# A transposed block's activations and remainders in one 512-column matmul, the halves added on VectorE

## The chip, the cores and the metric

The program runs on one core of one Trainium2 chip. The metric is the device time of that core in microseconds (us): 3461.25 us as the median of 3 runs of the kernel before. Engines are named as in the profile: PE is TensorE's matmul, PEld its weight load, DVE is VectorE, ACT is ScalarE, POOL is GpSimd, SP is SyncE, which only issues DMAs here.

## What is computed

Two transformer blocks on 256 tokens of width 2048, all in fp32. Cut to the matrix products that matter here:

```python
u = rms_norm(h, g_mix_pre) @ w_in               # 2048 x 5120: q, k, v, xr, yg
rec = rglru_bidirectional(xr, conv_w, ...) * gelu(yg)
s = einsum(q * HEAD_DIM ** -0.5, k) + bias      # attention of the first block
h = h + rms_norm(concat(norm(attn), norm(rec)) @ w_out)
ff = (silu(fn @ w_ffn_gate) * (fn @ w_ffn_up)) @ w_ffn_down      # 5632 hidden
...                                             # a gated embedding, then the second block
h2 = xn @ w_in_2; x = x + mixed @ w_out_2
qry = xn @ peer_w_query                         # routing: 16 of 16384 experts, 8 heads
act = gelu(xn . expert_down[idx])               # all 16384 experts are multiplied here
out = sum(gate * act * expert_up[idx])
```

The kernel doesn't gather experts: it multiplies the tokens with all 16384 rows of expert_down, applies gelu, multiplies by a gate that is zero for an expert not chosen, and multiplies with all of expert_up.

## The kernel before

Every weight matrix comes from one stream in memory of 1080 pieces, 128 x 1024 fp32 each (512 KB). A piece passes through four slots of `raw` (SP's DMA, L389 and L393), is rounded by ACT into four slots of `hi` (`take_hi`, L439), and its remainder raw - hi is taken by POOL into two slots of `lo`, in two halves of 512 columns (`take_lo`, L412). POOL waits for PE to have used the half piece two pieces back (`half_used`, `unit_used`), ACT for the piece four back, SP for POOL's `lo` of the same slot. So four half pieces of `lo` are all that lies between POOL and PE.

The activations are split too: `xh` is the rounded part, `xl` the remainder, each 128 x 16 x 256 (features on partitions, 16 blocks of features, 256 tokens). A product is three matmuls that add up in one PSUM bank (`exact`, L1619): rounded times rounded (L1622), rounded times remainder (L1623), remainder times rounded (L1624).

There are two kinds of use. A transposed block (`t_block`, L1646) makes 128 output features for 256 tokens: the weight is the loaded operand, the activations move, 256 columns; 16 feature blocks make 48 matmuls of 256 columns, from two pieces, and `ready` (L1643) waits for POOL four times in it, each time ahead of 12 matmuls. A natural piece (`n_piece`, L1667) has the activations as loaded operand and moves 512 columns of weights; `up_piece` (L2081) does so for the last stage, 12 matmuls of 512 columns for one piece.

The stages in order of the stream, with transposed blocks: `in1` 16 blocks (8 for xr, read by `block_copy` L961 on DVE, each followed by a four-tap convolution L975 and L978; 8 for yg, read by gelu on ACT), then 2 natural chunks for v, then 16 blocks m = 0 to 15 for q and k of the attention heads, copied by DVE (`qk_copy` L1007, q times SCALE) with attention between them; `out1` natural; `ffn` 88 blocks, a gate and an up block for each of 44 f, banks 2s and 2s+1; `down` and `gate` natural; `in2` 4 blocks (`t_copy` L1235), then natural; `out2` natural; `query` 16 blocks (L1452); `peer_down` 128 blocks; `peer_up` 256 natural pieces.

In `ffn`, ACT takes silu of the gate bank (L662) and DVE's `hidden` (L1179) multiplies the up bank by it (L1182), rounds it (L1185) and takes the remainder (L1189). In `peer_down`, ACT applies gelu to a block's bank (`expert_gelu` L843). From block GATE0 = 48 on, for 64 groups of four tokens, PE follows each block with 12 bf16 matmuls of 128 columns that build the gates (`gates_of`, L2018), and DVE makes the one-hot operands for the next group (`one_hots`, L1530), multiplies the block with the gates known so far (`gate_block` L1547) and the group's gates into all blocks (`gate_tokens` L1555). Blocks 112 to 127 have only `gate_block`. Each engine runs its own instructions in the order written; the order between engines is by semaphores.

## Time and profile before

| | value |
|---|---|
| median of 3 runs | 3461.25 us (3459.26 to 3461.52) |
| the profiled execution | 3463.77 us, of which the span is 3462.0 us |
| mean granted clock of TensorE | 0.976 of full |
| PE busy | 3273.0 us, 95% of the span, 21000 matmuls |
| PEld busy | 2955.1 us, 85% |
| POOL busy | 2905.4 us, 84% |
| ACT busy | 1508.1 us, 44% |
| DVE busy | 1079.3 us, 31% |
| memory read | 582.78 MB, 170 GB/s over the span |

The busy time of an engine is the union of its instructions' spans. A matmul's recorded span is its latency and overlaps with those of its neighbours, so what one matmul costs is read from the distance of starts, not from its duration. The profiled execution is 2.5 us above the median.

### The profile page before, as it was taken

To read this page: it belongs to the slowest core of one execution; us is meant where nothing else is said; L and a number is where in the kernel's file an instruction comes from. 1 tells how busy PE (TensorE), PEld (TensorE's weight loads), DVE (VectorE), ACT (ScalarE), POOL (GpSimd) and SP (SyncE) were. 2 spreads that over 40 slices of the span, in tenths; PEclk is the share of its full clock that TensorE was granted. 3 is DMA by queue.
4 is the path that set the end of the run, shared out by engine and by line. 5 is a ranking of instruction groups with operands and counts; after the bars stand their busy time and mean duration, and the time that the engine had idled before them with its cause. 6 is when DMAs were issued, how large, how long until landed. Compare 5 with 4: busy or idle time off the path is not lost.

```text
span 3462.0 us, 59974 instructions
## 1 busy us (share of the span) xinstructions
PE 3273.0 (95%) x21000; PEld 2955.1 (85%) x21000; DVE 1079.3 (31%) x1979; ACT 1508.1 (44%) x2006; POOL 2905.4 (84%) x2164
## 2 busy tenths in 40 slices
PE   7978989999999987999799998999999999999999
PEld 7868779999988866777578998999999988888887
DVE  6175132222200032344511264066665111111111
ACT  4734443333334344433334333433333455555554
POOL 6676878899989965898377889877888899999998
PEclk9999999999999999999899999999999999999999
DMA  6434545555555553554245554554445566566665
GB/s 203 154 113 133 173 137 182 183 181 183 182 192 194 192 171 113 170 166 150 79 153 181 173 172 146 184 162 162 163 161 167 193 191 192 193 193 194 193 191 180
DMA packets 159409, 588.40 MB, mean 170 GB/s; under 512 B 17840, under 2 KB 18096, under 8 KB 157904
## 3 DMA queue, kind: packets, MB, share of 16 engines
q1 hardware_dynamic: 156960, 570.50, 50.4%
q10 hardware_dynamic: 2352, 16.55, 1.3%
q8 instruction: 68, 1.11, 0.1%
q14 instruction: 29, 0.24, 0.0%
HBM read 582.78 MB, written 4.19 MB: 170 GB/s over the span
## 4 chain that ended last, share of the span: by engine, by line
PE 82%; DVE 3%; POOL 1%; ACT 1%; issue 1%; ACTq 0%; DVEq 0%; POOLq 0%
PE ps L1622 26%; PE ps L1624 26%; PE ps L1623 26%; PE ps L1685 3%; POOL lo L412 1%; PE ps L1680 1%; DVE hx L1170 1%; ACT xn L457 0%; PE ps L1741 0%; DVE at L1054 0%; DVE at L1066 0%; DVE small L1057 0%; DVE xn L922 0%; DVE xl L926 0%; DVE g L1256 0%
## 5 line engine op out<-in xcount | busy, mean ns | idle before, releaser
L412 POOL TENSOR_TENSOR lo<-raw,hi 128x512 fp32r<-128x512 f32 x2160 | 2905.2, 1359 | 546.3 <-PE ps L1624 322.7
L439 ACT ACTIVATE hi<-raw 128x1024 fp32r<-128x1024 f32 x1080 | 1128.3, 1059 | 1135.2 <-PE ps L1624 737.4
L1622 PE MATMUL ps<-xh,hi 128*128 128x256 f32 x4288 | 1226.2, 286 | 20.1 <-POOL lo L412 13.6
L1623 PE MATMUL ps<-xl,hi 128*128 128x256 f32 x4288 | 1215.4, 283 | 0.0
L1624 PE MATMUL ps<-xh,lo 128*128 128x256 f32 x4288 | 1215.0, 283 | 0.0
L1622 PEld LDWEIGHTS ps<-xh,hi 128*128 128x128 f32 x4288 | 824.9, 192 | 24.4 <-POOL lo L412 13.3
L1623 PEld LDWEIGHTS ps<-xl,hi 128*128 128x128 f32 x4288 | 825.0, 192 | 0.3
L1624 PEld LDWEIGHTS ps<-xh,lo 128*128 128x128 f32 x4288 | 824.9, 192 | 0.0
L1622 PE MATMUL ps<-hi,hg_h 128*128 128x512 f32 x1024 | 399.1, 390 | 3.9 <-POOL lo L412 3.9
L1624 PE MATMUL ps<-hi,hg_l 128*128 128x512 f32 x1024 | 399.0, 390 | 0.0
L1623 PE MATMUL ps<-lo,hg_h 128*128 128x512 f32 x1024 | 398.9, 390 | 0.0
L1622 PE MATMUL ps<-hi,xh 128*128 128x512 f32 x800 | 320.7, 401 | 27.8 <-POOL lo L412 16.4
L1623 PE MATMUL ps<-lo,xh 128*128 128x512 f32 x800 | 315.4, 394 | 0.0
L1624 PE MATMUL ps<-hi,xl 128*128 128x512 f32 x800 | 315.2, 394 | 0.0
L1622 PEld LDWEIGHTS ps<-hi,hg_h 128*128 128x128 f32 x1024 | 192.6, 188 | 44.1 <-issue 4.1
L1623 PEld LDWEIGHTS ps<-lo,hg_h 128*128 128x128 f32 x1024 | 192.6, 188 | 40.0
L1624 PEld LDWEIGHTS ps<-hi,hg_l 128*128 128x128 f32 x1024 | 192.5, 188 | 40.1
L1622 PEld LDWEIGHTS ps<-hi,xh 128*128 128x128 f32 x800 | 152.7, 191 | 71.6 <-POOL lo L412 22.2
L1624 PEld LDWEIGHTS ps<-hi,xl 128*128 128x128 f32 x800 | 152.4, 191 | 32.6
L1623 PEld LDWEIGHTS ps<-lo,xh 128*128 128x128 f32 x800 | 152.5, 191 | 31.5 <-issue 1.0
L847 ACT ACTIVATE ps<-ps 128x256 f32<-128x256 f32 (+32 forms) x79 | 22.4, 283 | 319.7 <-PE ps L1624 319.7
L894 ACT ACTIVATE hg_h<-gm 128x256 fp32r (+1 forms) x256 | 107.0, 418 | 93.4 <-PE ps L1624 91.8
(276 smaller groups left out, 2443.0 us busy)
## 6 DMA issues: line engine op xcount, KB each, us to landing
raw<-in_stream SPq DMA_DIRECT2D x1080, 512.0 KB, 3.4
gbc<-in_gains ACTq DMA_DIRECT2D x3, 1024.0 KB, 4.7
hx<-in_x SPq DMA_DIRECT2D x2, 1024.0 KB, 7.3
wg<-in_w_gates ACTq DMA_DIRECT2D x1, 2048.0 KB, 7.5
bias<-in_rpb ACTq DMA_DIRECT2D x1, 2048.0 KB, 8.1
w_pr<-in_w_proj ACTq DMA_DIRECT2D x1, 2048.0 KB, 7.7
spill<-hx ACTq DMA_DIRECT2D x1, 2048.0 KB, 7.5
hx_end<-spill ACTq DMA_DIRECT2D x1, 2048.0 KB, 7.9
```

The lines of the kernel that those rows point to most:

```text
L412: nc.gpsimd.tensor_tensor(lo[:, k % 2, n], raw[:, k, n], hi[:, k, n].bitcast(F32), ALU.subtract)\
L439: nc.scalar.activation(hi[:, k, :], raw[:, k, :], ACT.Copy).then_inc(hi_done, 1)
L847: ins = nc.scalar.activation(ps[:, bank, 0:n], ps[:, bank, 0:n], ACT.Gelu_apprx_tanh)
L894: nc.scalar.activation(hg_h[:, k, :], h, ACT.Copy).then_inc(hh_done, 1)
L1170: V.scalar_tensor_tensor(out=hx[:, tt], in0=y[:, tt], scalar=st(RI + tt), in1=hx[:, tt], op0=ALU.mult, op1=ALU.add)\
L1622: M.matmul(out_ap, a[0], b[0], start=start, stop=False)
L1623: M.matmul(out_ap, a[0], b[1], start=False, stop=False)
L1624: return M.matmul(out_ap, a[1], b[0], start=False, stop=stop)
L1680: ins = M.transpose(tr_slot(kb % 8)[:, tt * P:(tt + 1) * P], xn[:, tt, kb * P:(kb + 1) * P], ident)
L1685: return M.matmul(out_ap, a, b, start=start, stop=stop, **kw)
```

## The change

`xh` and `xl` become two views of one tile `xx`, 128 x 16 x 2 x 256, so that a feature block's rounded part and remainder lie side by side, 512 columns. In a wide `t_block` a feature block takes two matmuls instead of three: the rounded weight with all 512 columns into the whole bank, then the remainder weight with the 256 rounded columns into its first half. The bank then holds two halves that must be added: every reader of such a bank now begins with a `tensor_reduce` over two (512 elements read, 256 written) on DVE. Where DVE copied the bank before, the reduce takes the copy's place; in `ffn` and in the experts' blocks from 48 on it is added, into a free half or bank of PSUM, and ACT waits for it in place of PE (`gate_summed`, `down_summed`). PE waits for `down_summed` of four blocks back in place of gelu and `act_gated`. SCALE moves from q's copy to the addition of the bias (L1054), where `tensor_tensor` becomes `scalar_tensor_tensor`.

Wide are 8 blocks of `in1` (b < 8), 16 for q and k, 88 in `ffn`, 4 in `in2`, 16 in `query` and 80 in `peer_down` (48 to 127): 212 blocks. Not wide are the 8 gelu blocks of `in1` and the experts' blocks 0 to 47. The natural stages are as before.

```diff
-        xh = place("xh", [P, KB, T], X_AT, F32R)
-        xl = place("xl", [P, KB, T], X_AT + 16384, F32R)
+
+        xx = place("xx", [P, KB, 2, T], X_AT, F32R)
+        xh, xl = xx[:, :, 0, :], xx[:, :, 1, :]
...
+        def both_sums(b):
+            return ps[:, b, :].rearrange("p (a t) -> p t a", a=2)
+
+        def expert_sum(j):
+            return ps[:, 6, (j % 2) * T:(j % 2) * T + T]
...
-                act.wait_ge(unit_used, f * 4 + after("ffn", 2))
+                act.wait_ge(gate_summed, f + 1)
...
+                if isinstance(j, int) and j >= GATE0:
+                    act.wait_ge(down_summed, j - GATE0 + 1)
+                    n, v = gated_before(j), expert_sum(j)
...
+            def block_sum(b, to):
                 dve.wait_ge(unit_used, after("in1", 2 * b + 2))
...
+                V.tensor_reduce(to, both_sums(b % 4), AX.X, ALU.add).then_inc(free_d, 1)
...
             def hidden(f, s, first=False):
+                dve.wait_ge(unit_used, f * 4 + after("ffn", 2))
+                V.tensor_reduce(t_bank(4 + 2 * s), both_sums(2 * s), AX.X, ALU.add)\
+                    .then_inc(gate_summed, 1)
                 dve.wait_ge(unit_used, f * 4 + after("ffn", 4))
+                V.tensor_reduce(t_bank(5 + 2 * s), both_sums(2 * s + 1), AX.X, ALU.add)\
+                    .then_inc(up_summed, 1)
                 dve.wait_ge(free_a, f + 13)
+                dve.wait_ge(up_summed, f + 1)
...
+            def block_sums(j):
+
+                dve.wait_ge(unit_used, after("peer_down", 2 * j + 2))
+                if j >= GATE0 + 2:
+
+                    dve.wait_ge(free_a, 70 + j)
+                    dve.wait_ge(act_gated, max(j - 2 - GATE0, 0))
+                V.tensor_reduce(expert_sum(j), both_sums(j % 4), AX.X, ALU.add)\
+                    .then_inc(down_summed, 1)
...
             for m in range(GROUPS):
+                block_sums(GATE0 + m)
                 if m + 1 < GROUPS:
                     one_hots(m + 1)
...
+            def pair(i_, b_, w_h, w_l, first, last):
+
+                M.matmul(ps[:, b_, :], w_h, xx[:, i_].rearrange("p a t -> p (a t)"), start=first,
+                         stop=False)
+                return M.matmul(t_bank(b_), w_l, xh[:, i_, :], start=False, stop=last)
...
-                        ins = exact(t_bank(bank), w, (xh[:, kb, :], xl[:, kb, :]), T,
-                                    kb == 0, kb == KB - 1)
+                        if wide:
+                            ins = pair(kb, bank, *w, kb == 0, kb == KB - 1)
```

## Rows read from the trace of the kernel before

**Rows 1.** The page: busy times; the chain that ended last, shares by line.

```profile
PE 3273.0 (95%) x21000; PEld 2955.1 (85%) x21000; DVE 1079.3 (31%) x1979; ACT 1508.1 (44%) x2006; POOL 2905.4 (84%) x2164
...
PE ps L1622 26%; PE ps L1624 26%; PE ps L1623 26%; PE ps L1685 3%; POOL lo L412 1%; PE ps L1680 1%; DVE hx L1170 1%; ACT xn L457 0%; PE ps L1741 0%; DVE at L1054 0%; DVE at L1066 0%; DVE small L1057 0%; DVE xn L922 0%; DVE xl L926 0%; DVE g L1256 0%
```

**Rows 2.** Windows: us, length, each engine's busy time (instructions), clock, DMA share, GB/s.

```profile
500.00:900.00 400.00, 400.00 (x3336) 400.00 (x3335) 98.68 (x105) 156.86 (x175) 360.08 (x279) 1.00 0.55 182
1000.00:1200.00 200.00, 200.00 (x884) 165.58 (x884) 2.58 (x4) 80.23 (x82) 190.19 (x148) 1.00 0.58 192
...
2350.00:2650.00 300.00, 300.00 (x2776) 298.02 (x2775) 197.26 (x372) 109.14 (x186) 238.81 (x186) 1.00 0.49 162
```

**Rows 3.** Timeline of DVE in ffn: start us, length us, instruction, [idle before <-releaser].

```profile
500.79 0.42 DVE L1182 TENSOR_TENSOR prod<-ps,sil 128x256 f32<-128x256 f32 x1 [8.44 <-ACT sil L662]
...
512.31 0.42 DVE L1182 TENSOR_TENSOR prod<-ps,sil 128x256 f32<-128x256 f32 x1 [8.44 <-ACT sil L662]
```

**Rows 4.** Timeline of DVE in peer_up, eight pieces in a row, first and last.

```profile
2765.34 0.42 DVE L1570 TENSOR_TENSOR hg_l<-gm,hg_h 128x256 fp32r<-128x256 f32 x1 [2.31 <-ACT hg_h L894]
...
2784.38 0.42 DVE L1570 TENSOR_TENSOR hg_l<-gm,hg_h 128x256 fp32r<-128x256 f32 x1 [2.29 <-ACT hg_h L894]
```

**Rows 5.** Instruction groups by line and form: count, busy us, mean ns, idle before.

```profile
L1622 PEld LDWEIGHTS ps<-xh,hi 128*128 128x128 f32 x4288 | 824.9, 192 | 24.4 <-POOL lo L412 13.3 <-DVE xl L926 7.4 <-ACT gm L852 1.7
...
L1057 DVE TENSOR_REDUCE small<-at 128x2 f32<-128x512 f32 x20 | 13.7, 686 | 0.7
...
L1509 DVE TENSOR_REDUCE route<-pick 128x256 f32<-128x4096 f32 x2 | 8.8, 4420 | 0.1
...
L1452 DVE COPY qry_t<-ps 128x256 f32<-128x256 f32 x16 | 6.8, 425 | 83.3 <-PE ps L1624 83.3
...
L1054 DVE TENSOR_TENSOR at<-ps,bias 128x512 f32<-128x512 f32 x8 | 5.5, 692 | 4.3 <-PE ps L1685 4.3
```

**Rows 6.** Timeline of POOL in four stretches: start, length, count of operations.

```profile
31.71 41.59 POOL L412 TENSOR_TENSOR lo<-raw,hi 128x512 fp32r<-128x512 f32 x30 [8.69 <-ACT hi L439]
...
194.24 27.44 POOL L412 TENSOR_TENSOR lo<-raw,hi 128x512 fp32r<-128x512 f32 x15
...
509.56 2.68 POOL L412 TENSOR_TENSOR lo<-raw,hi 128x512 fp32r<-128x512 f32 x2 [0.21 <-PE ps L1624]
...
1329.73 5.30 POOL L412 TENSOR_TENSOR lo<-raw,hi 128x512 fp32r<-128x512 f32 x4 [3.37 <-PE ps L1624]
```

**Rows 7.** Timeline of the gated stage, one round: PE's gates and DVE's work.

```profile
2452.85 0.84 PE L1685 MATMUL ps<-hot_j,hot_i 128*128 128x128 bf16 x12
...
2453.73 0.69 DVE L1535 TENSOR_TENSOR hot_i<-ps,i_t 128x512 bf16<-128x512 f32 x1 [2.27 <-PE ps L1685]
...
2457.45 0.50 DVE L1564 COPY gm<-ps 128x192 f32<-128x192 f32 x1
...
2459.34 0.84 PE L1685 MATMUL ps<-hot_j,hot_i 128*128 128x128 bf16 x12
```

**Rows 8.** Timelines where the end of a block is waited for: DVE and PE.

```profile
224.01 0.42 DVE L967 TENSOR_SCALAR q_t<-ps 128x256 f32<-128x256 f32 x1
...
231.67 5.57 PE L1685 MATMUL ps<-th_i,cons_sb 128*128 128x256 f32 x16 [11.49 <-DVE th_i L1043]
...
971.77 0.42 DVE L1182 TENSOR_TENSOR prod<-ps,sil 128x256 f32<-128x256 f32 x1 [7.10 <-PE ps L1624]
...
1943.74 3.84 PE L1685 MATMUL ps<-keys_t,qry_t 128*128 128x128 f32 x32 [0.52 <-DVE qry_t L1452]
...
2757.36 0.47 PE L1622 MATMUL ps<-hi,hg_h 128*128 128x512 f32 x1 [3.89 <-POOL lo L412]
```

**Rows 9.** Timeline of DVE in the attention stage, one head's second half.

```profile
269.66 2.37 DVE L1073 TENSOR_SCALAR at<-at,small 128x256 f32<-128x256 f32 x2
273.31 0.42 DVE L965 COPY k_t<-ps 128x256 f32<-128x256 f32 x1 [1.27 <-PE ps L1624]
```

**Rows 10.** Timeline of DVE in the convolution, the last block.

```profile
75.01 0.41 DVE L965 COPY xr<-ps 128x256 f32<-128x256 f32 x1
```

More of the change, by code:

```diff
@@ L195, in build @@
         hid_hi = sem("hid_hi")
+        gate_summed, up_summed, down_summed = (sem(n) for n in (
+            "gate_summed", "up_summed", "down_summed"))
         out_stored = sem("out_stored")
@@ L657, in silu @@
             def silu(f, s):
[L659 removed]
+                act.wait_ge(gate_summed, f + 1)
                 act.wait_ge(prod_done, f - 1) if not isinstance(f, int) or f >= 2 else None
[L662 removed]
+                nc.scalar.activation(sil[:, s, :], t_bank(4 + 2 * s), ACT.Silu).then_inc(free_a, 1)
             def ffn_pair(f0, r, first=False, last=False):
@@ L843, in expert_gelu @@
             def expert_gelu(j, bank):
-                act.wait_ge(unit_used, j * 2 + after("peer_down", 2))
-                n = gated_before(j) if isinstance(j, int) else 0
+                if isinstance(j, int) and j >= GATE0:
+                    act.wait_ge(down_summed, j - GATE0 + 1)
+                    n, v = gated_before(j), expert_sum(j)
+                else:
+                    act.wait_ge(unit_used, j * 2 + after("peer_down", 2))
+                    n, v = 0, t_bank(bank)
                 if n:
-                    ins = nc.scalar.activation(ps[:, bank, 0:n], ps[:, bank, 0:n],
-                                               ACT.Gelu_apprx_tanh)
+                    ins = nc.scalar.activation(v[:, 0:n], v[:, 0:n], ACT.Gelu_apprx_tanh)
                 if n < T:
@@ L851, in expert_gelu @@
                         gm[:, bass.ds(j, 1), :].rearrange("p a t -> p (a t)")
-                    ins = nc.scalar.activation(to, ps[:, bank, n:T], ACT.Gelu_apprx_tanh)
+                    ins = nc.scalar.activation(to, v[:, n:T], ACT.Gelu_apprx_tanh)
                 ins.then_inc(free_a, 1)
@@ L1007, in qk_copy @@
             def qk_copy(m):
-                block_copy(24 + m, (q_t, k_t)[m % 2][:, m // 2, :], None if m % 2 else SCALE)
+                block_sum(24 + m, (q_t, k_t)[m % 2][:, m // 2, :])
             def scan(z):
@@ L1053, in first @@
                         dve.wait_ge(at_e, n - 1)
-                    V.tensor_tensor(s_sb[:, h % 2], ps[:, 4 + h % 2, :].rearrange(
-                        "p (a b) -> p a b", a=2), bias_of(h), ALU.add).then_inc(at_b, 1)
+                    V.scalar_tensor_tensor(
+                        out=s_sb[:, h % 2], in0=ps[:, 4 + h % 2, :].rearrange(
+                            "p (a b) -> p a b", a=2), scalar=SCALE if times is None else 1.0,
+                        in1=bias_of(h), op0=ALU.mult, op1=ALU.add).then_inc(at_b, 1)
                     dve.wait_ge(at_b, n + 1)
@@ L1581, in _ @@
             for j in range(GATE0 + GROUPS, NKEY):
+                block_sums(j)
                 gate_block(j)
@@ L1706, in _ @@
                     pe.wait_ge(free_d, b - 3)
-                t_block(b // 2, 2 * (b % 2), b % 4, norm=0 if b == 0 else None)
+                t_block(b // 2, 2 * (b % 2), b % 4, norm=0 if b == 0 else None, wide=b < 8)
                 if b in (9, 11, 13, 15):
@@ L2003, in _ @@
             for j in range(4):
-                t_block(r0 + j // 2, 2 * (j % 2), j)
+                t_block(r0 + j // 2, 2 * (j % 2), j, wide=False)
             with pe.Fori(1, 3) as i:
@@ L2031, in gates_of @@
                 ins.then_inc(gmat_done, 1)
-            def bank_gated(i, j):
-                pe.wait_ge(act_gated, i * 4 + (j - 4 - GATE0))
             pe.wait_ge(routed, 1)
             g0 = GATE0 // 4
-            down_blocks(g0, gates_of)
-            for j in range(4):
-                if j:
-                    bank_gated(g0 + 1, j)
-                pe.wait_ge(free_a, 71 + 4 * (g0 + 1) + j - 3)
-                t_block(2 * (g0 + 1) + (r0 + j // 2), 2 * (j % 2), j)
-                gates_of(g0 + 1, j)
-            with pe.Fori(g0 + 2, g0 + GROUPS // 4) as i:
-                down_blocks(i, gates_of, bank_gated)
+            down_blocks(g0, gates_of, True)
+            with pe.Fori(g0 + 1, g0 + GROUPS // 4) as i:
+                down_blocks(i, gates_of, True, True)
             with pe.Fori(g0 + GROUPS // 4, 32) as i:
-                down_blocks(i, None, bank_gated)
+                down_blocks(i, None, True, True)
             def up_piece(i, k, half, first=False, last=False):
```

38 lines of the change are left out of this document (17 added, 21 removed).

## The prediction

> **What bounds the kernel now.** First the page's busy times and the chain that ended last [rows 1]: PE is busy 95% of the span, and the three lines of `exact` carry 78% of the chain, so the time is PE's time plus few stalls. POOL stands at 84% and is the next engine, so it has to be watched. Then the windows by stage [rows 2]: in `ffn`, `down` and the gated part of `peer_down` PE is busy for the whole of the window at full clock. There the distance between matmul starts sets the time, and that comes from periods, not from recorded durations (a few records are missing, so a count in a window is slightly low).
>
> One f of `ffn` is 96 matmuls of 256 columns, and DVE's product comes back after 512.31 - 500.79 = 11.52 us [rows 3], so a matmul of 256 columns costs 11.52 / 96 = 120.0 ns, a block 48 x 0.120 = 5.76 us. In `peer_up` seven pieces of 12 matmuls of 512 columns take 2784.38 - 2765.34 = 19.04 us [rows 4], so one of 512 costs 19.04 / 84 = 226.7 ns. Doubling the columns adds 106.7 ns, and 13.3 ns are left over at either length: the step from one loaded operand to the next has a price that doesn't depend on the columns.
>
> **What a wide block saves.** Per feature block 3 x 120.0 = 360.0 ns becomes 226.7 + 120.0 = 346.7 ns: 13.3 ns, and 16 x 13.3 = 0.213 us for a block, 5.76 to 5.547 us. The number of columns that stream is the same (768), so only the fixed part of one matmul in three goes. 212 blocks give 45.2 us. The trace of before has no row of the two lengths in turn; the sum takes each at the price that it has among its own kind. The load itself is hidden in both streams: its record is 192 ns long [rows 5] and the starts are 120 ns apart. If the fixed part vanished at one of the two changes, a feature block would cost 333.3 ns and the gain double, until POOL stops it (below); if the load showed behind the short matmul, it is the slower rival.
>
> The Trainium skill, "TensorE: Matmul & The Clock Gate", section "Back-to-back issue gap", gives a warm gap of N / 2.4 + 2.5 ns. By that, a merged matmul saves 2.5 ns and not 13.3, an estimate of 3392 x 2.5 = 8.5 us for the whole change. The trace disagrees with the 2.5: it shows 13.3 over 213.3 at 512 columns. It is rival 2.
>
> **Does POOL keep up?** A wide block needs four `lo` halves in 5.547 us, 1.387 us each, where they had 1.44. In `ffn` POOL runs two in 2.68 us and then waits 0.21 for PE [rows 6], so PE sets its pace. Left alone it does four in 5.30 us, 1.325 each; beside the convolution, where DVE works on SBUF without pause, 30 in 41.59, 1.386 each; beside the wide scans 15 in 27.44, 1.83 each [rows 6]. In `ffn` DVE is busy 98.7 of 400 us [rows 2], and what the change adds there reads and writes PSUM, so POOL lies between 1.325 and 1.386, and 1.387 is just enough. In `down` PE's quarter is 6 x 0.2267 = 1.36 us, shorter than that, and PE is busy all through [rows 2]; memory gives 192 GB/s there, and a wide block asks for 2 x 0.524 MB / 5.547 us = 189. ACT's rounding has the same pace as in `down`. So the cover holds, with some 4% to spare.
>
> **What DVE pays.** A reduce of 512 elements takes 686 ns, where a copy took 425 [rows 5]; 4096 elements into 256 sums take 4420, the same 1.04 us per 1000 read elements, so the number of sums costs nothing. I take 0.69. The reads here are strided and none of the rows is, so the upper end is 1.39 (each element at twice the time), the lower one the copy's 0.42. The addition with SCALE reads the same 512 elements as L1054 (692 ns) and I cost it at nothing.
>
> Where DVE is beside the path:
> - Gated blocks. PE's gates run from 2452.85, DVE's `hot_i` begins at 2453.73 after 2.27 us of idleness, because it waits for the gates, and the round's last piece ends at 2457.95, 5.10 us after PE ended the block; the next block ends at 2459.34, after 6.49 [rows 7]. `block_sums` stands ahead of `one_hots` and runs in the 0.88 us in which DVE waits for the gates anyway. Round after: 6.49 - 0.21 = 6.28, DVE's chain 5.1 (5.6 at a reduce of 1.39). Covered. Gelu comes 0.7 us later, and behind it in ACT's queue stands the rounding of the two pieces of the block after next; PE needs the first of them one round (6.28 us) later, ACT is busy only 109 of 300 us here [rows 2], and POOL has a round of its own for four halves (4 x 1.39 = 5.6 us). No wait on PE follows.
> - `ffn`. The gate reduce ends five us before ACT comes to silu (DVE waits 8.44 us for silu's result [rows 3]); the up reduce runs while ACT still rounds a piece. PE waits for silu and `hidden` of two f back. Nothing.
> - Convolution. DVE has no idle before the last block's copy [rows 10]; with 0.26 more per block its pace is slower than PE's, by the last block some 1 us. The first reader of the convolution on PE comes two blocks (11 us) later. Nothing.
> - Attention. After DVE has scaled a head's probabilities (269.66 + 2.37 = 272.03) 1.27 us pass before the block's end at 273.3, when PE turns them [rows 9]. The block is 0.21 shorter, and a q sum that ends 0.26 later stands ahead of the head's chain in DVE's queue, if DVE doesn't wait for the scores there anyway. 1.27 - 0.21 - 0.26 = 0.8 is left. Nothing.
>
> Where it is on the path:
> - Before the sum of squares PE waits 11.49 us for DVE, and the q and k copies lie in DVE's queue ahead of it [rows 8]: 2 x 0.26 = 0.52 us. That wait also swallows the savings of blocks m = 0, 1, 2: 3 x 0.213 = 0.64 us.
> - The last k block of attention and the last block of `query` (PE waits 0.52 for its copy [rows 8]): 2 x 0.26 = 0.52.
> - End of `ffn`: the product starts with the block's end at 971.77 [rows 8]; now a reduce and its semaphore stand before it: 0.75. End of `peer_down`: PE is idle 3.89 us, on the chain gelu, gate, round, remainder [rows 8]; the sum ahead of it: 0.75.
>
> Sum: 45.2 - 0.64 - 0.52 - 0.52 - 1.50 = 42.0 us. Span 3462.0 to 3420.0, the profiled execution 3463.8 to 3421.8; it lies 2.5 above the median, so the median is 3461.25 - 42.0 = 3419. With the reduce at 1.39 the six places cost 0.70 more each, 4.2 us: 3423. At 0.42: 3418.
>
> **Rivals.**
> 1. POOL becomes the pace in the wide blocks. For it: 1.386 beside a busy DVE, and only 0.06 us of slack. Against: PE never waits for it in `down` at 1.36. At 1.41 us per half, 848 halves save 0.03 each: 25.4 - 3.2 = 22 us, 3439. Chance 0.07.
> 2. Only 2.5 ns of a merged matmul are saved, since the rest follows the columns: 8.5 - 3.2 = 5 us, 3456, no change. Against: the periods at both lengths. Likewise if the new sums ate the gain elsewhere. Chance 0.03.
> 3. Slower: the load behind the short matmul. The 512-column matmul's weight is loaded while one of 256 columns runs. If a load is hidden today only because matmuls of equal length are queued closely, and it must run for its 192 ns [rows 5] from the short one's start, a feature block costs 192 + 226.7 = 419 ns, 59 more than now: 3392 x 0.059 = 199 us, 3660. It decides from 133 ns of exposed load upward. Against: starts stand 120 ns apart today with a new load each time. Chance 0.02.
> 4. The fixed part goes at both changes: 90 us by PE, but POOL's 1.325 x 4 = 5.30 us allows 0.46 per block, 97, so the gain is 88: 3374. Chance 0.03.
>
> The forecast itself has 0.85. Beside the costs above it is uncertain by the stretches at a lower clock after stalls (mean clock 0.976), which may shift by a few us. Its own range is 3413 to 3427; I take in part of rival 1: 3412 to 3432.
>
> What measurement can tell from no change is about 0.2%, 6.9 us. Faster by more: 0.85 + 0.07 + 0.03 = 0.95, less a little for mishaps, 0.94. Within: 0.03. Slower: 0.03.
>
> **What would show each step.** In the profile after, DVE's products in `ffn` should stand 11.09 us apart, PE busy for the whole window, POOL's idle between pairs of halves 0.1 instead of 0.21. If they stand 11.3 apart and PE waits for POOL, it is rival 1; 11.5, rival 2; 13, rival 3. The new reduces should read 0.69 us (L1452's successor). The gated round should be 6.28 us with `hot_i` still waiting for PE's gates. The waits for DVE before the sum of squares should be some 1.2 us longer, the gap at the end of `ffn` 0.75 longer. The prediction is wrong if the two lengths in turn cost other than the mean of their kinds, or if a reduce over two strided halves costs more than 1.4 us.

## The result and the profile after

The kernel after takes 3434.93 us, the median of 4 runs (3430.34 to 3435.99), beside 3461.39 us for the kernel before: a ratio of 0.992, 95% interval 0.991 to 0.994. It is faster by 26.5 us; 42 were predicted, and the time lies outside the predicted range of 3412 to 3432. The profiled execution took 3434.05 us, its span 3432.3, 29.7 below the 3462.0 of before. That is 3.2 us more than the medians differ by, since the profiled execution of before lies 2.4 above its median and that of after 0.9 below its own.

The page of the kernel after, as in [rows 1]: busy times, the chain by line, and the two groups of the merged pair (L1661 is the matmul of 512 columns, L1663 the one of 256).

```profile
PE 3240.0 (94%) x17608; PEld 2764.5 (81%) x17608; DVE 1334.9 (39%) x2147; ACT 1495.1 (44%) x2006; POOL 2875.1 (84%) x2164
...
PE ps L1661 20%; PE ps L1652 16%; PE ps L1654 15%; PE ps L1653 15%; PE ps L1663 10%; PE ps L1724 3%; POOL lo L423 1%; DVE hx L1181 1%; PE ps L1719 0%; DVE xx L940 0%; ACT xn L468 0%; PE ps L1780 0%; DVE at L1063 0%; DVE at L1077 0%; DVE small L1068 0%
...
L1661 PE MATMUL ps<-xx,hi 128*128 128x512 f32 x3392 | 1202.6, 398 | 8.0 <-DVE xx L940 6.4
L1663 PE MATMUL ps<-xx,lo 128*128 128x256 f32 x3392 | 950.9, 280 | 0.0
```

PE has 3392 matmuls fewer (21000 to 17608), 3392 in either group of the pair, and still bounds the kernel. The windows that answer to [rows 2], with the same columns:

```profile
500.00:900.00 400.00, 400.00 (x2267) 346.92 (x2266) 143.24 (x176) 160.18 (x177) 365.95 (x284) 1.00 0.57 186
1000.00:1200.00 200.00, 200.00 (x884) 165.61 (x883) 3.86 (x6) 80.10 (x84) 190.31 (x148) 1.00 0.59 194
2350.00:2650.00 300.00, 300.00 (x2087) 263.01 (x2086) 227.78 (x413) 112.23 (x190) 246.61 (x193) 1.00 0.52 168
```

PE is busy for the whole of each window at full clock, as before, so again the distance of starts counts. That is read from DVE's timeline, which answers to [rows 3]. L1192 sums the gate bank and L1195 the up bank in `ffn`, each right after its block; L1580 is the sum in `peer_down`, here in its last 16 blocks.

```profile
500.17 0.70 DVE L1192 TENSOR_REDUCE ps<-ps 128x256 f32<-128x512 f32 x1 [1.21 <-PE ps L1663]
505.82 0.70 DVE L1195 TENSOR_REDUCE ps<-ps 128x256 f32<-128x512 f32 x1 [4.95 <-PE ps L1663]
...
511.48 0.70 DVE L1192 TENSOR_REDUCE ps<-ps 128x256 f32<-128x512 f32 x1 [1.21 <-PE ps L1663]
...
2684.16 0.70 DVE L1580 TENSOR_REDUCE ps<-ps 128x256 f32<-128x512 f32 x1 [3.99 <-PE ps L1663]
...
2689.70 0.70 DVE L1580 TENSOR_REDUCE ps<-ps 128x256 f32<-128x512 f32 x1 [3.99 <-PE ps L1663]
...
2695.25 0.70 DVE L1580 TENSOR_REDUCE ps<-ps 128x256 f32<-128x512 f32 x1 [3.99 <-PE ps L1663]
```

This is the finding of the case. In `ffn` a block takes 5.65 us (505.82 - 500.17, and 11.31 for two), 353.3 ns for a feature block. In the last 16 blocks of `peer_down` the same two matmuls over the same operands take 5.55 us (11.09 for two), 346.7 ns, which is the predicted price. The distances between matmul starts, worked out from the trace's records, show how the two differ:

```
ns from one start to the next, kernel after (512 = the 512-column matmul is running)
ffn, from 699.60 us:         512: 241  256: 120  512: 236  256: 113  512: 233  256: 117  then again
peer_down, from 2689.85 us:  512: 230  256: 117  512: 230  256: 117  512: 230  256: 117
q and k, from 253.43 us:     512: 231  256: 112  512: 233  256: 117  then again
before, ffn:                 256: 120  256: 120  256: 120
```

The long rhythm repeats with every third feature block, 1060 ns, 353.3 each. The short price comes in two forms, one that repeats with every feature block and one, in many blocks of q and k, that repeats with every second; the mean is 346.7 ns in both. Below, short means either of these. The mean over a stage, worked out from the same starts, tells which price it kept (before: 360.0). Distances behind other matmuls are left out, on which the value for q and k hangs by up to 1 ns; its blocks from the fourth on stand at 346.7. Of the gated blocks the first two stand at 353.3, the other 62 at 346.7 but for one wider distance at each start.

| stage (wide blocks) | ns for a feature block, kernel after | predicted |
|---|---|---|
| `in1` (8) | 353.1 | 346.7 |
| q and k, with attention (16) | 347.7 | 346.7 |
| `ffn` (88) | 353.3 | 346.7 |
| `in2` (4) | 353.4 | 346.7 |
| `query` (16) | 353.2 | 346.7 |
| `peer_down`, gated (64) | 347.2 | 346.7 |
| `peer_down`, last 16 | 346.7 | 346.7 |

In 116 of the 212 blocks 16 x 6.66 = 107 ns of the predicted 213 are missing: 12.4 us, and 42.0 - 12.4 = 29.6 is the difference of the two spans, 29.7 (26.5 between the medians).

### The profile page after: what moved, and what is told of

It reads as the page before. It is cut to its first block, busy times and chain, and to the rows that moved or that the text cites. A ratio compares the mean times of both kernels' runs of the same rounds, so it can differ in the third digit from the quotient of the medians.

```text
span 3432.3 us, 53383 instructions
## 1 busy us (share of the span) xinstructions
PE 3240.0 (94%) x17608; PEld 2764.5 (81%) x17608; DVE 1334.9 (39%) x2147; ACT 1495.1 (44%) x2006; POOL 2875.1 (84%) x2164
## 4 chain that ended last, share of the span: by engine, by line
PE 81%; DVE 3%; POOL 1%; ACT 1%; issue 1%; ACTq 0%; DVEq 0%; POOLq 0%
PE ps L1661 20%; PE ps L1652 16%; PE ps L1654 15%; PE ps L1653 15%; PE ps L1663 10%; PE ps L1724 3%; POOL lo L423 1%; DVE hx L1181 1%; PE ps L1719 0%; DVE xx L940 0%; ACT xn L468 0%; PE ps L1780 0%; DVE at L1063 0%; DVE at L1077 0%; DVE small L1068 0%
## 5 line engine op out<-in xcount | busy, mean ns | idle before, releaser
L423 POOL TENSOR_TENSOR lo<-raw,hi 128x512 fp32r<-128x512 f32 x2160 | 2874.8, 1338 | 547.0 <-ACT hi L450 208.0
L1661 PE MATMUL ps<-xx,hi 128*128 128x512 f32 x3392 | 1202.6, 398 | 8.0 <-DVE xx L940 6.4
L1663 PE MATMUL ps<-xx,lo 128*128 128x256 f32 x3392 | 950.9, 280 | 0.0
L1661 PEld LDWEIGHTS ps<-xx,hi 128*128 128x128 f32 x3392 | 636.5, 188 | 159.3 <-DVE xx L940 7.4
L1663 PEld LDWEIGHTS ps<-xx,lo 128*128 128x128 f32 x3392 | 641.0, 189 | 0.2
L1652 PE MATMUL ps<-hi,xx 128*128 128x512 f32 x800 | 320.5, 401 | 27.7 <-POOL lo L423 16.3
L1654 PE MATMUL ps<-hi,xx 128*128 128x512 f32 x800 | 314.8, 394 | 0.0
L1653 PE MATMUL ps<-lo,xx 128*128 128x512 f32 x800 | 314.7, 393 | 0.0
L1652 PE MATMUL ps<-xx,hi 128*128 128x256 f32 x896 | 256.7, 287 | 11.4 <-POOL lo L423 11.4
L1653 PE MATMUL ps<-xx,hi 128*128 128x256 f32 x896 | 255.3, 285 | 0.0
L1654 PE MATMUL ps<-xx,lo 128*128 128x256 f32 x896 | 255.2, 285 | 0.0
L1654 PEld LDWEIGHTS ps<-hi,hg_l 128*128 128x128 f32 x1024 | 192.7, 188 | 40.1
L1652 PEld LDWEIGHTS ps<-hi,xx 128*128 128x128 f32 x800 | 152.4, 190 | 71.5 <-POOL lo L423 22.5
L1598 DVE TENSOR_TENSOR hg_l<-gm,hg_h 128x256 fp32r<-128x256 f32 x128 | 124.2, 971 | 220.2 <-ACT hg_h L908 220.2
L1621 DVE TENSOR_TENSOR hg_l<-gm,hg_h 128x256 fp32r<-128x256 f32 x128 | 121.5, 949 | 224.3 <-ACT hg_h L908 224.3
```

The lines of the kernel that those rows point to most:

```text
L423: nc.gpsimd.tensor_tensor(lo[:, k % 2, n], raw[:, k, n], hi[:, k, n].bitcast(F32), ALU.subtract)\
L1598: V.tensor_tensor(hg_l[:, k, :], h, hg_h[:, k, :].bitcast(F32), ALU.subtract)\
L1621: V.tensor_tensor(hg_l[:, k, :], gm[:, bass.ds(i * 4 + (k - NKEY), 1), :].rearrange("p a t -> p (a t)"), hg_h[:, k, :].bitcast(F32), ALU.s ...
L1652: M.matmul(out_ap, a[0], b[0], start=start, stop=False)
L1653: M.matmul(out_ap, a[0], b[1], start=False, stop=False)
L1654: return M.matmul(out_ap, a[1], b[0], start=False, stop=stop)
```

## What the other rows show

The gated stage, as in [rows 7]: PE's gates, DVE's sum, `hot_i` (L1553), the next round's sum.

```profile
2400.44 0.84 PE L1724 MATMUL ps<-hot_j,hot_i 128*128 128x128 bf16 x12
...
2400.64 0.70 DVE L1580 TENSOR_REDUCE ps<-ps 128x256 f32<-128x512 f32 x1 [1.44 <-PE ps L1663]
2401.32 0.69 DVE L1553 TENSOR_TENSOR hot_i<-ps,i_t 128x512 bf16<-128x512 f32 x1
...
2406.93 0.70 DVE L1580 TENSOR_REDUCE ps<-ps 128x256 f32<-128x512 f32 x1 [1.45 <-PE ps L1663]
```

The round is 2406.93 - 2400.64 = 6.29 us (6.28 predicted, 6.49 before). The sum waits 1.44 us for the block and runs beside the gates; `hot_i` begins 0.88 us after PE's gates began, as it did before.

The places where a block's end is waited for, as in [rows 8]: the first reduce of q, the matmul after the scans, the last `hidden` of `ffn` and the first matmul of `down`, the one after `query` and the first of `peer_up`.

```profile
222.44 0.69 DVE L978 TENSOR_REDUCE q_t<-ps 128x256 f32<-128x512 f32 x1
...
230.63 2.93 PE L1724 MATMUL ps<-th_i,cons_sb 128*128 128x256 f32 x6 [12.04 <-DVE th_i L1052]
...
958.09 0.70 DVE L1195 TENSOR_REDUCE ps<-ps 128x256 f32<-128x512 f32 x1 [4.95 <-PE ps L1663]
958.82 0.42 DVE L1199 TENSOR_TENSOR prod<-ps,sil 128x256 f32<-128x256 f32 x1
...
961.95 0.79 PE L1652 MATMUL ps<-hi,hid_h 128*128 128x512 f32 x1 [3.89 <-DVE hid_l L1206]
...
1930.02 2.16 PE L1724 MATMUL ps<-keys_t,qry_t 128*128 128x128 f32 x17 [0.78 <-DVE qry_t L1469]
...
2727.57 0.77 PE L1652 MATMUL ps<-hi,hg_h 128*128 128x512 f32 x1 [4.62 <-POOL lo L423]
```

The sum of q at 222.44 stands 1.57 us earlier than the copy of before, the matmul behind it 1.04 earlier: the two longer readers cost 0.53, where 0.52 was predicted. The wait after `query` is 0.78 where it was 0.52, and the one ahead of `peer_up` 4.62 where it was 3.89: +0.26 and +0.73 (0.26 and 0.75 predicted). In `ffn` the last product begins 0.73 after the start of the sum, and PE's wait ahead of `down` is 3.89 where it was 3.07 before, +0.82 (0.75 predicted):

```profile
974.71 0.49 PE L1622 MATMUL ps<-hi,hid_h 128*128 128x512 f32 x1 [3.07 <-DVE hid_l L1189]
```

The sums themselves (count, busy us, mean ns):

```profile
L1580 DVE TENSOR_REDUCE ps<-ps 128x256 f32<-128x512 f32 x80 | 56.0, 700 | 241.0 <-PE ps L1663 241.0
...
L1469 DVE TENSOR_REDUCE qry_t<-ps 128x256 f32<-128x512 f32 x16 | 11.1, 691 | 77.6 <-PE ps L1663 77.6
```

0.69 to 0.70 us, as taken. And POOL in `ffn`, as in [rows 6]:

```profile
696.73 2.65 POOL L423 TENSOR_TENSOR lo<-raw,hi 128x512 fp32r<-128x512 f32 x2 [0.18 <-PE ps L1663]
```

It waits 0.18 us for PE between pairs. PE sets the pace and POOL follows, so rival 1 is out by this row for `ffn`. It holds in one short stretch: beside the wide scans POOL has no idle time at all, and PE waits for it in the first three blocks of q and k.

```profile
192.69 27.42 POOL L423 TENSOR_TENSOR lo<-raw,hi 128x512 fp32r<-128x512 f32 x15
...
213.66 0.50 PE L1661 MATMUL ps<-xx,hi 128*128 128x512 f32 x1 [1.47 <-POOL lo L423]
```

At 1.83 us a half four halves take 7.3 us, more than a block at either price, and these three blocks took 20.8 us before and after the change (199.34 to 220.18 and 197.78 to 218.59 us).

Where the 29.7 us arose, from the start times of the same instructions in both traces:

| stretch | predicted | measured |
|---|---|---|
| up to the first product of `ffn` | 3.7 | 4.4 |
| `ffn` | 18.0 | 8.4 |
| `down`, `gate`, `in2`, `out2` | 0.9 | -0.5 |
| `query` | 3.1 | 1.4 |
| routing, up to the first gates | 0 | 1.4 |
| gated `peer_down` | 13.6 | 12.0 |
| its last 16 blocks and the turn to `peer_up` | 2.7 | 2.7 |
| `peer_up` | 0 | -0.1 |

More than half of the missing time is in `ffn`.

## The experiments

The open question was why the pair has two prices, and whether the halves, the sums, POOL or the mix of lengths is behind it. All edits are made to the kernel after. The letters in the expectations are those of the hypotheses named there. No kernel leaves out work.

**1. The halves and sums without the mix.** A feature block is again three matmuls of 256 columns, but into the two halves, with all sums kept.

```diff
-                M.matmul(ps[:, b_, :], w_h, xx[:, i_].rearrange("p a t -> p (a t)"), ...)
+                M.matmul(t_bank(b_), w_h, xh[:, i_, :], start=first, stop=False)
+                M.matmul(ps[:, b_, T:2 * T], w_h, xl[:, i_, :], start=False, stop=False)
                 return M.matmul(t_bank(b_), w_l, xh[:, i_, :], start=False, stop=last)
```

> The changed kernel with the wide pair taken back to three matmuls of 256 columns that fill the two halves of the bank; all of DVE's new sums stay. It prices the sums alone. Both theories of the matmul's pace expect 120.0 ns each, so 11.52 us for an f of ffn and 5.76 for a block of query. The prediction's terms say: 0.5 us later by the sum of squares, 0.3 more by the end of attention and by the end of query, 0.75 at the end of ffn and of peer_down, in all 2.5 to 3.2 us above the kernel before, some 3464. If the sums cost more than that, as a rival has it, the span is 3470 or more. If the output's half were what costs 6.7 ns, an f would take 11.7 us or more.

3462.2 us, span 3460.4. DVE's sums in `ffn`:

```profile
700.52 0.70 DVE L1192 TENSOR_REDUCE ps<-ps 128x256 f32<-128x512 f32 x1 [1.25 <-PE ps L1669]
...
706.28 0.70 DVE L1195 TENSOR_REDUCE ps<-ps 128x256 f32<-128x512 f32 x1 [5.06 <-PE ps L1669]
```

A block is 5.76 us, as before the change. The time is a single execution, 2.0 us above the median of the kernel before in the same rounds (3460.2, from 3458.1 to 3463.0), so by itself it doesn't tell the expected 2.5 to 3.2 us from nothing. PE's waits for a reader do: in this run they are 12.02, 0.35, 3.78, 0.78 and 4.62 us (behind the scans, behind the last k block, and ahead of `down`, of routing and of `peer_up`) where before they were 11.49, 0.08, 3.07, 0.52 and 3.89, together 2.5 us more. So halves and sums cost these 2.5 us at the fixed places and nothing in the blocks; what is missing of the gain lies in the matmuls.

**2. Both matmuls of 512 columns.** The second one takes the remainders too, which adds the products of remainder with remainder to the result.

```diff
-                return M.matmul(t_bank(b_), w_l, xh[:, i_, :], start=False, stop=last)
+                return M.matmul(ps[:, b_, :], w_l, xx[:, i_].rearrange("p a t -> p (a t)"),
+                                start=False, stop=last)
```

> The changed kernel with the second matmul of a pair 512 columns wide too (the remainder weight also meets the remainders, and the whole bank is added up), so that a wide block is one stream of equal lengths. If a matmul of 512 columns costs 226.7 ns with this operand order as in the natural stages, and only the change of length costs more, a feature block takes 453.3 ns, a block of ffn or query 7.25 us, and the whole some 3434 + 3392 x 0.1 = 3773 less what the overlap gives. If a matmul of 512 columns in a transposed block costs 233.3 ns (the grouped kernel's quarter of 1.403 us is 4 x 233.3 + 4 x 117.5), a feature block takes 466.7 and a block 7.47 us: then the price of 512 that the prediction took from the natural stages was the wrong one.

3769.9 us.

```profile
502.49 0.70 DVE L1192 TENSOR_REDUCE ps<-ps 128x256 f32<-128x512 f32 x1 [4.02 <-PE ps L1663]
...
509.74 0.70 DVE L1195 TENSOR_REDUCE ps<-ps 128x256 f32<-128x512 f32 x1 [6.55 <-PE ps L1663]
```

A block takes 7.25 us for 32 matmuls, 226.7 ns each, as expected if 512 columns cost the same as in the natural stages, and so read the starts too. The price of 512 columns, taken from `peer_up` [rows 4], holds in a transposed block. With 120.0 for three of 256 (experiment 1) both prices of a kind are right in place; only the mix costs more than their mean.

**3. Grouped by four, then by eight.** In a quarter block the four 512-column matmuls come first and the four of 256 after, or eight and eight per piece; the number of changes of length falls from two a feature block to two in four or in eight.

```diff
                         if wide:
-                            ins = pair(kb, bank, *w, kb == 0, kb == KB - 1)
+                            M.matmul(ps[:, bank, :], w[0], xx[:, kb]..., start=kb == 0, stop=False)
+                            if j % 4 == 3:
+                                for jj in range(j - 3, j + 1):
+                                    kk = 8 * half + jj
+                                    ins = M.matmul(t_bank(bank), lo[:, k % 2, jj * P:(jj + 1) * P],
+                                                   xh[:, kk, :], start=False, stop=kk == KB - 1)
```

> The changed kernel with the two lengths not in turn but grouped: for each quarter of a block four matmuls of 512 columns, then the four of 256. Theory A: the missing gain (353.3 ns for a feature block where 346.7 was forecast, in in1, ffn, in2 and query) is a price of each change between the two lengths. Then grouping takes three changes in four away: 348 ns or less, an f of ffn in 11.15 us or less where the changed kernel takes 11.31, and the whole kernel some 6 us faster, 3429. Theory B: it comes from how PE and POOL meet in those stages, whatever the order: then an f stays at 11.31 us and the whole at 3435. Theory C: the price is of changing the loaded operand between hi and lo: then an f is shorter too, as in A; the first pair of the group tells A and C apart.

> The grouped kernel with groups of eight: eight matmuls of 512 columns, then eight of 256, so one change of length in eight. If the changes of length cost (theory A), a block takes 5.58 us or less, where groups of four take 5.61, and the whole some 3426. If a matmul of 512 costs 233.3 ns and one of 256 117.5 here whatever their neighbours (16 x 350.8), it stays at 5.61 us and the whole at 3428. POOL gets its halves back later and in pairs; if that tells, blocks vary and PE waits for POOL.

By four: 3428.1 us (3427.9 to 3428.5, 4 runs), ratio 0.991 [0.989, 0.992]. Its sums in `ffn`:

```profile
702.41 0.70 DVE L1192 TENSOR_REDUCE ps<-ps 128x256 f32<-128x512 f32 x1 [1.18 <-PE ps L1685]
...
708.02 0.70 DVE L1195 TENSOR_REDUCE ps<-ps 128x256 f32<-128x512 f32 x1 [4.92 <-PE ps L1685]
...
713.63 0.70 DVE L1192 TENSOR_REDUCE ps<-ps 128x256 f32<-128x512 f32 x1 [1.19 <-PE ps L1685]
```

5.61 us, 350.8 ns a feature block, and the same in `in1`, `in2`, `query` and the last blocks of `peer_down`. By eight: 3427.2 us (3424.5 to 3432.0, 4 runs), ratio 0.991 [0.990, 0.993]; two blocks in `ffn` take 712.32 - 701.03 = 11.29, in which DVE's reading of the end is uneven, and the mean over starts is 349.2 ns:

```profile
701.03 0.70 DVE L1192 TENSOR_REDUCE ps<-ps 128x256 f32<-128x512 f32 x1 [0.29 <-PE ps L1686]
...
712.32 0.70 DVE L1192 TENSOR_REDUCE ps<-ps 128x256 f32<-128x512 f32 x1 [0.40 <-PE ps L1686]
```

```
ns from start to start, ffn
by four:   512: 233 236 228 233                    256: 117 119 117 117
and then:  512: 235 233 236 224                    256: 118 120 120 120
by eight:  512: 233 236 228 233 231 226 227 227    256: 113 119 120 120 120 120 120 120
```

By eight, after a change to 512 columns the first five matmuls stand up to 9 ns wider than 226.7, then the pace of the kind is reached; after the change back the first two are up to 7 ns closer than 120. So a change of length has an echo over several matmuls, and a stream that changes more often doesn't come to the end of it. Grouping helped, but less than the expectation of a price per change had it: an f takes 11.22 us by four, where 11.15 or less was expected. It is not a price per change: two changes cost 4 x (350.8 - 346.7) = 16 ns by four and 8 x (349.2 - 346.7) = 20 by eight, but in strict alternation 0 or 7.

**4. What puts a stage into the long rhythm?** Three probes in one kernel: `in1` begins with two blocks of three matmuls, a single fp32 matmul stands ahead of each up block of `ffn`, and in `query` ACT waits for DVE's sum, so that POOL's pace is set by ACT.

```diff
+                    M.matmul(ps[:, 2 * s + 1, 0:P], ident, ident, start=True, stop=True)
                     t_block(i * 2 + (r0 + s), 2, 2 * s + 1)
...
                     take_hi(i + ROUND0["query"], k)
+                    if k % 2:
+                        act.wait_ge(free_d, i * 2 + (95 + k // 2))
```

> Three changes to the changed kernel in three stages that don't meet. in1: the first two blocks are three matmuls of 256 columns each, so that the wide blocks are entered from a stream of 256 as in peer_down. ffn: one fp32 matmul of 128 columns on its own ahead of each up block. query: ACT waits for DVE's sum of a block before it rounds the next pieces, as gelu makes it do in peer_down. Theory B1 (PE stays in the state in which it entered): in1's wide blocks fall from 5.65 to 5.55 us, query stays at 5.65. Theory B2 (an interruption resets it): the up blocks of ffn fall to 5.55. Theory B3 (POOL tied to PE's release slows PE, POOL late by ACT doesn't): query's blocks fall to 5.55 and in1 stays at 5.65. Theory A (each change of length costs): all stay at 5.65, which doesn't explain 5.55 in peer_down.

3447.3 us. In `ffn`:

```profile
704.81 0.70 DVE L1197 TENSOR_REDUCE ps<-ps 128x256 f32<-128x512 f32 x1 [5.17 <-PE ps L1665]
...
710.46 0.70 DVE L1194 TENSOR_REDUCE ps<-ps 128x256 f32<-128x512 f32 x1 [1.19 <-PE ps L1665]
...
716.33 0.70 DVE L1197 TENSOR_REDUCE ps<-ps 128x256 f32<-128x512 f32 x1 [5.17 <-PE ps L1665]
```

The gate block takes 5.65 us, the up block with its extra matmul 5.87: 353.3 ns a feature block still, and so in `in1` (353.4) and `query` (353.3). None of B1, B2 and B3 came true: all 44 up blocks behind an fp32 matmul have the long rhythm. For the other two probes this is one execution each of a thing that can vary (below).

**5. bf16 matmuls ahead of a few blocks.** The stages that keep the short rhythm have bf16 matmuls between blocks (the gates) or other matmuls (attention). Twelve bf16 matmuls of 128 columns, whose output nobody reads, go ahead of two blocks of `in1`, two of `ffn` and three of `query`, seven bursts in all.

```diff
+            def burst(bank):
+                one = ident.bitcast(BF16)[:, 0:P]
+                for _ in range(12):
+                    M.matmul(ps[:, bank, 0:P], one, one, start=True, stop=True)
...
+                    if first:
+                        burst(2 * s + 1)
                     t_block(i * 2 + (r0 + s), 2, 2 * s + 1)
```

> The changed kernel with a burst of 12 bf16 matmuls of 128 columns (the form of the gates) ahead of two blocks of in1, of the first two up blocks of ffn and of three blocks of query, nothing else. Theory D: the wide stream has two steady rhythms, 353.3 and 346.7 ns for a feature block, and what stands ahead of it decides which; once entered it stays, which is how peer_down's last 16 blocks go on at 346.7 without gates. Then after one of the bursts the blocks of that stage fall from 5.65 to 5.55 us and stay there: ffn 9 us shorter. Theory E: only a stage's other work (the gates in every round, the heads of attention) holds the faster rhythm, or it is a property of the stage: then the blocks after the bursts stay at 5.65.

3424.9 us, span 3423.1.

```profile
701.80 0.70 DVE L1192 TENSOR_REDUCE ps<-ps 128x256 f32<-128x512 f32 x1 [1.15 <-PE ps L1663]
...
707.35 0.70 DVE L1195 TENSOR_REDUCE ps<-ps 128x256 f32<-128x512 f32 x1 [4.85 <-PE ps L1663]
...
712.90 0.70 DVE L1192 TENSOR_REDUCE ps<-ps 128x256 f32<-128x512 f32 x1 [1.15 <-PE ps L1663]
```

After its two bursts `ffn` runs all its blocks at 5.55 us, 346.7 ns: what happened in the first two f lasts for 470 us. By the starts a burst costs 0.74 us (0.65 of its own, the rest in the distances at its ends). With seven of them (5.2 us) taken off, this execution lies 40.1 us below the median of before in the same rounds (3459.7): with the short price in most stages the predicted 42.0 come out, within 2 us.

**6. Bursts in every long stage, one burst alone, bursts of one.** The first also has bursts in `in2`; the second has a single burst, ahead of `ffn`'s first up block; the third is experiment 5 with one matmul in each burst.

```diff
-                for _ in range(12):
+                for _ in range(1):
```

> The changed kernel with the burst of 12 bf16 matmuls ahead of two blocks in each of in1, ffn, in2 and query, as a version to keep. Eight bursts cost 8 x 0.74 = 5.9 us (less where PE would wait anyway). Theory D (two rhythms, the faster one entered after a burst and kept): ffn's 88 blocks win 0.107 us each, 9.4 in all, in1, in2 and query 28 blocks 3.0, so the time is 3434.9 + 5.9 - 12.4 = 3428, and an f of ffn takes 11.09 us. If which rhythm a stage takes were chance from execution to execution, the spread of its times would be as wide as the changed kernel's (3430 to 3436).

> The changed kernel with one burst only, ahead of the first up block of ffn. Theory D expects an f of 11.09 us where it took 11.31, for 43 f's 9.4 us, less 0.74 for the burst: 3434.9 - 8.7 = 3426; query and in1 stay as they are, at 5.65 us a block. If it needs two bursts, as the gates needed two rounds, ffn stays at 11.31 and the time at 3435.7.

> The kernel of e5 with bursts of one bf16 matmul instead of twelve, at the same seven places. If any change of the kind of matmul starts the stream anew, the faster rhythm follows here too: ffn's f 11.09 us, the whole 3425 - 5 = 3420. If it takes a longer stretch of other work (an fp32 matmul of 128 columns on its own, in e3, didn't do it), ffn stays at 11.31 and the whole at 3435.

3430.4 us (3425.8 to 3436.4, 4 runs), 3425.4 us (3421.9 to 3431.5, 4 runs) and 3421.7 us (a single run). The profiled execution of the second:

```profile
699.49 0.70 DVE L1195 TENSOR_REDUCE ps<-ps 128x256 f32<-128x512 f32 x1 [4.95 <-PE ps L1663]
...
705.15 0.70 DVE L1192 TENSOR_REDUCE ps<-ps 128x256 f32<-128x512 f32 x1 [1.21 <-PE ps L1663]
```

`ffn` stayed at 5.65 us in spite of its burst, in the first of the three as well. In the third, with single bf16 matmuls, it had the short one. So the expectation that a burst settles the rhythm is wrong for two kernels of three. The median of the second, 3425.4, is nevertheless the expected 3426: the profiled execution, 3431.5, is the longest of its four, and in the others, of which there is no profile, `ffn` may have been short.

**7. The same kernels again.** The kernel after unaltered, and that of experiment 5 unaltered, in five rounds.

> The changed kernel itself, unaltered, beside the three above. If the rhythm of a stage is fixed by the program, this profile shows 5.65 us a block in in1, ffn, in2 and query again and 5.55 in peer_down's last 16, and times of 3434 to 3436. If it is partly chance, a stage has changed sides: query at 5.55 would take 1.7 us off, ffn at 11.09 us for an f 9.4.

> The kernel of e5_bursts once more, nothing altered, timed in five rounds. Theory D with chance (the rhythm of a stage is decided anew in each execution, and a burst only shifts the odds): the executions scatter between 3422 and 3436, over more than 5 us, and the profiled one may show ffn at 5.65 us a block although e5's showed 5.55. Rival, the bursts decide it for good: all executions lie within 3 us of 3424, and ffn stands at 5.545 us a block, query's second half at 5.545.

The kernel after: 3433.8 us (3432.9 to 3439.1, 4 runs), ratio 0.993 [0.991, 0.995], with the same rhythm in the same stages. The kernel of experiment 5: 3432.0 us (3425.2 to 3445.9, 6 runs). Its rows in `ffn` and in `query`:

```profile
700.15 0.70 DVE L1195 TENSOR_REDUCE ps<-ps 128x256 f32<-128x512 f32 x1 [4.85 <-PE ps L1663]
...
705.70 0.70 DVE L1192 TENSOR_REDUCE ps<-ps 128x256 f32<-128x512 f32 x1 [1.15 <-PE ps L1663]
...
1877.35 0.69 DVE L1469 TENSOR_REDUCE qry_t<-ps 128x256 f32<-128x512 f32 x1 [5.70 <-PE ps L1663]
...
1883.00 0.69 DVE L1469 TENSOR_REDUCE qry_t<-ps 128x256 f32<-128x512 f32 x1 [4.96 <-PE ps L1663]
```

`ffn` has the short rhythm again, but `query`, which ran at 5.55 us a block in experiment 5, keeps 5.65 after all its three bursts. The same instructions in the same order gave another rhythm in another execution. It ran on another chip, so the two profiles alone don't part the execution from the chip; the four executions of the kernel with one burst, all on one chip, lie up to 9.6 us apart, where `ffn`'s rhythm is worth 9.4. What was said of chance holds as far as the times scatter over more than 5 us; what was not foreseen are two executions of 3445 us, above anything the kernel after gave; there is no profile of them.

| ns a feature block, profiled execution | `in1` | q, k | `ffn` | `in2` | `query` | gated | last 16 |
|---|---|---|---|---|---|---|---|
| after | 353.1 | 347.7 | 353.3 | 353.4 | 353.2 | 347.2 | 346.7 |
| after, again | 353.3 | 348.4 | 353.3 | 353.4 | 353.3 | 347.2 | 346.7 |
| seven bursts | 348.0 | 347.5 | 346.7 | 352.7 | 346.7 | 347.2 | 346.7 |
| seven bursts, again | 353.3 | 348.8 | 346.7 | 352.7 | 353.3 | 347.2 | 346.7 |
| seven bursts of one | 349.7 | 348.9 | 346.7 | 353.4 | 347.3 | 347.2 | 346.7 |
| bursts in all long stages | 347.9 | 349.0 | 353.3 | 346.9 | 347.3 | 347.2 | 346.7 |
| one burst | 353.1 | 348.2 | 353.3 | 353.2 | 353.3 | 347.2 | 346.7 |

The starts of these seven executions show when a rhythm is chosen. In no stretch of pairs in unbroken turn at the full granted clock does the price change; where it changes, another matmul, a wait or a stretch at the lower clock stands between. Behind the 30 bursts (seven of them of one matmul) the long rhythm follows 11 times and the short one 19 times, and it is there from the block right behind the burst. Behind the gates it is the long one in the second gated block and the short one in all 62 that follow, in all seven.

**8. Every second pair mirrored.** Odd feature blocks take the 256-column matmul first: 512 256 256 512 512 256 256 512, one change of length a feature block.

```diff
+                            if kb % 2:
+                                ins = mirrored(kb, bank, *w, kb == KB - 1)
+                            else:
+                                ins = pair(kb, bank, *w, kb == 0, False)
```

> Odd feature blocks take the 256-column matmul first and the 512-column one second, so that lengths come as 512 256 256 512 512 256 256 512: one change of length per feature block where the changed kernel has two. If each change of length costs (grouped by four: 16 ns over the sum of kinds for two changes, grouped by eight 20 ns, so 8 to 10 a change), a feature block takes 346.7 + 8 to 10 = 355 to 357 ns in every wide stage, a block 5.7 us, and the run 3440 +- 4. If what costs is only the strict alternation falling into its slow rhythm of three feature blocks, the mirrored order cannot fall into it: 346.7 to 350.8 ns everywhere, blocks of 5.55 to 5.61 us, 3421 to 3429.

3423.7 us (3422.2 to 3425.9, 4 runs), ratio 0.9891 [0.9876, 0.9906]. It gains 37.0 us on the median of before in the same rounds, where the kernel after gained 26.5 and 25.2, and its interval lies, narrowly, below both of that kernel's (0.9907 to 0.9938 and 0.9914 to 0.9947). Sums in `ffn` and in the last blocks of `peer_down`:

```profile
704.76 0.70 DVE L1195 TENSOR_REDUCE ps<-ps 128x256 f32<-128x512 f32 x1 [4.88 <-PE ps L1667]
...
710.34 0.70 DVE L1192 TENSOR_REDUCE ps<-ps 128x256 f32<-128x512 f32 x1 [1.16 <-PE ps L1667]
...
715.91 0.70 DVE L1195 TENSOR_REDUCE ps<-ps 128x256 f32<-128x512 f32 x1 [4.88 <-PE ps L1667]
...
2680.97 0.70 DVE L1580 TENSOR_REDUCE ps<-ps 128x256 f32<-128x512 f32 x1 [4.01 <-PE ps L1667]
...
2686.54 0.70 DVE L1580 TENSOR_REDUCE ps<-ps 128x256 f32<-128x512 f32 x1 [4.01 <-PE ps L1667]
```

5.573 us a block in either stage, 348.4 ns a feature block. The starts are 236 116 113 232 231 113 120 233 ns in turn, a pattern of four feature blocks; every wide stage shows it or its mean (348.3 to 348.9) in this one profile. The gain is 212 x (5.76 - 5.573) = 39.6, less the 3.2 of the fixed costs, 36.5 us; 37.0 was measured (3460.72 to 3423.69). The expectation by a price per change (355 to 357 ns, 3440 us) is refuted, the one by the rhythms is met.

## Why the prediction was wrong

The direction, the mechanism and all terms but one held:

- The price of a kind, 120.0 and 226.7 ns: right, in place too (experiments 1 and 2).
- The price of the pair in turn, 346.7 ns: right in most of 96 blocks, 353.3 in the other 116, which is 12.4 us of the 42.0. This is the step that failed. It took the two lengths in turn at the mean of their kinds, said that no row of before shows them in turn, and named this as what would make it wrong; but the range, 13 us above the forecast, left it no room. The bounds that [rows 3] and [rows 4] allow were 333.3 and 360.0 ns, so that anything between no gain and twice the gain was open.
- POOL keeps up: right outside the scans. In `ffn` its halves take 1.32 to 1.33 us, at the lower end of the predicted 1.325 to 1.386, and it still waits for PE.
- DVE's sums, 0.69: right. What lay beside the path stayed there: experiment 1 has all sums, and PE's waits grew at the places named and by 2.5 us in all.
- The six fixed places: 0.53 for the first q and k, 0.27 for the last k block, 0.26 for `query`, 0.82 for the end of `ffn` and 0.73 for that of `peer_down`, 2.6 together where 2.54 was predicted. The wait before the sum of squares grew by 0.55 us (11.49 to 12.04) where 1.2 was predicted. The 0.64 for blocks m = 0, 1, 2 wasn't there to be had: they run beside the wide scans, where POOL's 1.83 us a half [rows 6] sets the pace, and took 20.8 us before and after. The sum isn't touched by it, since it took the 0.64 out again.
- Gated rounds: 6.29 us for 6.28; the stage as a whole gave 12.0 us, not 13.6.
- Rival 1 is out (POOL waits for PE in `ffn`; its sign, products 11.3 us apart, came true, but PE never waited for POOL there), rival 2 is out (the period is not 5.76), rivals 3 and 4 are out (no stage at 419 or 333 ns). The truth lay between forecast and rival 2, and no case stood there.

The Trainium skill, "TensorE: Matmul & The Clock Gate", section "Back-to-back issue gap", has N / 2.4 + 2.5 ns, and calls it the gap of an isolated matmul. From it the prediction worked out an estimate of 8.5 us; the trace shows 13.3 ns over the columns' time in the fp32 streams, and the change gained 26.5 us. The section gives the gap by a matmul's own columns and nothing for a change of length, so it has neither of the rhythms.

What is left open: what in the hardware makes the rhythms, and so why the pair costs 353.3 ns in one stage and 346.7 in another. Shown is that both prices exist at the full granted clock (1.00 in the windows of `ffn` and of `peer_down`, 2.4 GHz), with PE never waiting for another engine in these windows, that an unbroken stream keeps the one it has, that the same kernel took another one in another execution, and that other orders of the lengths gave other prices (348.4, 349.2, 350.8). Whether bf16 matmuls ahead of a block raise the odds of the short one isn't settled: `ffn` had it in three of five profiled executions with them, and in none of three without. The times lean the same way: 8 of the 16 executions with bursts took less than 3430 us, and none of the 8 of the kernel after; only five of the 16 were profiled.

## What to carry to other kernels

A price read from a uniform stream is not its price in a mixed one: here the mix stood at the mean of its kinds in some stages and 6.6 ns above it in others. Where a change puts two shapes in turn, keep the range open between the two prices that the uniform streams allow, and measure the mix first. When a stream alternates between two lengths, try the orders that have fewer changes (mirrored pairs, or groups): here the mirrored order was worth another 11 us or so and groups of four or eight another 6 to 7, for a change of a few lines. The four executions by four lie within 0.6 us and the mirrored ones within 3.7, where those of the kernel after span 5.7 and 6.2. And read a period in every stage in which an instruction stream occurs, since the same stream can have two prices, and take the profile of more than one execution before a stage's pace is called that of the kernel.

## What was not expected of the hardware

- Two steady prices of one instruction stream, 353.3 and 346.7 ns a feature block, the latter in two patterns of starts, and an echo of a change of length over five matmuls (233, 236, 228, 233, 231 ns, then 226.7).
- DVE's remainder in `peer_up` (128 x 256 fp32 in SBUF), untouched by the change, took 448 ns before and 971 after. But it isn't the change that did it: the kernel of seven bursts has 971 in experiment 5 and 448 in experiment 7, with the same instructions on every engine (on two chips, but the chip of experiment 7 shows 970 for the kernel after too). The kernel after, then these two:

```profile
L1598 DVE TENSOR_TENSOR hg_l<-gm,hg_h 128x256 fp32r<-128x256 f32 x128 | 124.2, 971 | 220.2 <-ACT hg_h L908 220.2
```

```profile
L1598 DVE TENSOR_TENSOR hg_l<-gm,hg_h 128x256 fp32r<-128x256 f32 x128 | 124.2, 971 | 220.3 <-ACT hg_h L908 220.3
```

```profile
L1598 DVE TENSOR_TENSOR hg_l<-gm,hg_h 128x256 fp32r<-128x256 f32 x128 | 57.2, 448 | 286.0 <-ACT hg_h L908 286.0
```

Where DVE takes 971 ns, POOL's halves in `peer_up` average 1308 ns, and where it takes 448 they average 1397. Here too one program has two patterns, and which one an execution shows isn't explained. DVE waits for ACT either way (220 and 286 us idle before these), so it cost nothing here.
